# Order of the vector work around a seven-product down projection: two layers of a Trainium2 block stack

## The reference, cut to what matters

```python
def conv_ffn(h, w_up, conv_w, conv_b, w_down):
    up = h @ w_up
    a, bval = up[..., :D_FF], up[..., D_FF:]
    a = causal_conv3(a, conv_w) + conv_b
    return (jax.nn.silu(a) * bval) @ w_down      # 512 x 2816 by 2816 x 1024

for l in range(2):
    h = rms_norm(x, norm_mix[l]); proj = h @ w_in[l]
    ...                                          # attention, x = x + mixed @ w_out[l]
    h = rms_norm(x, norm_ffn[l])
    x = x + conv_ffn(h, w_up[l], conv_w[l], conv_b[l], w_down[l])
return rms_norm(x, norm_final)
```

## Time and profile before

| | us |
|---|---|
| median of three runs | 2137.65 |
| the profiled execution | 2137.98 |
| its span, first to last instruction | 2136.1 |
| TensorE busy in it | 2104.3 |
| VectorE busy in it | 1434.2 |
| ScalarE busy in it | 833.5 |

### The profile page before, as it was taken

How to read it: one execution, slowest core, us unless ns; L and a number is a source line. 1 busy time by engine, 2 the same in 40 slices (tenths; PEclk the granted TensorE clock), 3 DMA queues, 4 the chain that set the end, 5 groups by cost and what they waited for, 6 DMA issues and landing times.

```text
span 2136.1 us, 25152 instructions
## 1 busy us (share of the span) xinstructions
PE 2104.3 (99%) x10183; PEld 1733.5 (81%) x10183; DVE 1434.2 (67%) x1880; ACT 833.5 (39%) x1092; POOL 40.4 (2%) x67
## 2 busy tenths in 40 slices
PE   7999999999999999999999999999999999999998
PEld 4888888888888887888888888788788888888876
DVE  6899897953665748634856666964853476666696
ACT  3323232322352345344353333444544435333344
POOL 1000000000000100000000000000000000000000
PEclk9999999999999999999999999999999999999999
DMA  9432322332332232322234433853232223443385
GB/s 312 153 119 84 99 91 97 99 102 96 99 104 97 101 99 79 119 79 77 93 109 148 135 130 140 318 192 99 79 119 79 80 99 120 142 141 125 141 308 196
DMA packets 188855, 272.28 MB, mean 127 GB/s; under 512 B 5052, under 2 KB 154436, under 8 KB 187972
## 3 DMA queue, kind: packets, MB, share of 16 engines
q1 hardware_dynamic: 178432, 221.01, 30.8%
q0 software_dynamic: 4192, 27.84, 3.7%
q10 hardware_dynamic: 6116, 21.82, 2.7%
HBM read 244.96 MB, written 25.69 MB: 127 GB/s over the span
## 4 chain that ended last, share of the span: by engine, by line
PE 92%; DVE 5%; ACT 1%; issue 1%; DMA 0%; POOL 0%; SPq 0%; POOLq 0%; ACTq 0%; DVEq 0%
PE psum L2126 29%; PE psum L2128 29%; PE psum L2127 29%; DVE whl L577 1%; PE psum L2625 1%; PE psum L2657 1%; PE psum L2637 1%; PE psum L2355 1%; DMA ada<-in_w_ada 0%; PE psum L2580 0%; PE psum L2610 0%; PE psum L2596 0%; DVE mrow L1974 0%; PE psum L2150 0%; ACT hT L988 0%
## 5 line engine op out<-in xcount | busy, mean ns | idle before, releaser
L2126 PE MATMUL psum<-hT,whl 128*128 128x512 f32 (+1 forms) x2064 | 789.1, 382 | 2.7 <-DVE whl L577 1.4
L2128 PE MATMUL psum<-hT,whl 128*128 128x512 f32 (+1 forms) x2064 | 783.1, 379 | 0.0
L2127 PE MATMUL psum<-hT,whl 128*128 128x512 f32 (+1 forms) x2064 | 783.0, 379 | 0.0
L577 DVE TENSOR_TENSOR whl<-raw,whl 128x1024 fp32r<-128x1024 f32 x361 | 437.3, 1214 | 264.7 <-ACT whl L570 264.5
L570 ACT ACTIVATE whl<-raw 128x1024 fp32r<-128x1024 f32 x361 | 376.8, 1048 | 334.1 <-PE psum L2128 287.8
L2126 PEld LDWEIGHTS psum<-hT,whl 128*128 128x128 f32 x2064 | 388.1, 188 | 83.1 <-issue 6.7
L2128 PEld LDWEIGHTS psum<-hT,whl 128*128 128x128 f32 x2064 | 388.2, 188 | 73.5
L2127 PEld LDWEIGHTS psum<-hT,whl 128*128 128x128 f32 x2064 | 388.3, 188 | 71.7 <-issue 0.2
L2126 PE MATMUL psum<-whl,hT 128*128 128x512 f32 (+1 forms) x320 | 112.2, 351 | 1.9 <-DVE whl L577 1.9
L2127 PE MATMUL psum<-whl,hT 128*128 128x512 f32 (+1 forms) x320 | 111.0, 347 | 0.0
L2128 PE MATMUL psum<-whl,hT 128*128 128x512 f32 (+1 forms) x320 | 111.0, 347 | 0.0
(11 more groups left out here) (346 smaller groups left out, 2561.5 us busy)
## 6 DMA issues: line engine op xcount, KB each, us to landing
raw<-in_w_in SPq DMA_DIRECT2D x87, 1024.0 KB, 5.1
raw<-in_w_up SPq DMA_DIRECT2D x44, 1024.0 KB, 6.2
raw<-in_w_down SPq DMA_DIRECT2D x22, 1024.0 KB, 5.6
s_by_pair<-sstage POOLq DMA_DIRECT2D x22, 768.0 KB, 4.1
ff_r<-s_by_pair ACTq DMA_DIRECT2D x22, 768.0 KB, 6.5
raw<-in_w_branch SPq DMA_DIRECT2D x12, 1024.0 KB, 5.1
raw<-in_w_out SPq DMA_DIRECT2D x12, 1024.0 KB, 5.0
raw<-in_w_down SPq DMA_DIRECT2D x20, 512.0 KB, 5.5
```

The lines of the kernel that those rows point to most:

```text
L577: nc.vector.tensor_tensor(whl_view(w, 1), raw_view(w), whl_view(w, 0).bitcast(F), ALU.subtract).then_inc(w_lo, 1)
L2126: M(out_, stat_hi, mov_hi, start=start, stop=False, **kw)
L2127: M(out_, stat_hi, mov_lo, start=False, stop=False, **kw)
L2128: return M(out_, stat_lo, mov_hi, start=False, stop=stop, **kw)
```

## The change

It has five parts. The last pair's token sums leave the loop over `f2` and go between the stage's later pieces, on VectorE and on ScalarE. The two adds of banks 6 and 7 go ahead of `split_lo` of sD2. The order of splits and norm steps between the layers changes on both engines. TensorE's transposes of token block 3 go behind the first half tile of sq0 in layer 1, as they already did in layer 0. In the last row `statistics` moves ahead of the multiplication by the gain.

```diff
 # ScalarE, norm(s), s != 2
                     norm_hi(s, 0)
-                    if s != 4:
+                    if s == 4:
+                        split_hi(w0 + 4)
+                        scaled(s, 2)
+                        split_hi(w0 + 5)
+                        norm_hi(s, 1)
+                    else:
                         norm_sum(s, 2)
-                    scaled(s, 2)
-                    norm_hi(s, 1)
-                    split_hi(w0 + 4)
-                    split_hi(w0 + 5)
+                        ...
                     norm_sum(s, 3)
                     scaled(s, 3)
                     norm_hi(s, 2)
                     split_hi(w0 + 6)
                     split_hi(w0 + 7)
 # ScalarE, end of a turn of f2; tokens_hi and sums_hi hold the lines as they were
-                    act.wait_ge(s_sums, 2 * (PAIRS * l + f2) + 1)
-                    ...
+                    if f2 < PAIRS - 1:
+                        tokens_hi(f2)
+                        sums_hi(f2)
 # ScalarE, the stage
                 for w in range(W[("sB", l, 0)], W[("sD", l, 0)] + 1):
                     split_hi(w + 3)
+                    if key_of[w] == ("sB", l, 2):
+                        tokens_hi(PAIRS - 1)
+                        sums_hi(PAIRS - 1)
                     if key_of[w] in back_at:
                         sums_back(back_at[key_of[w]])
 # VectorE, gain0 and statistics (last layer only)
-                    step(V.tensor_scalar(ms0[:, tb:tb + 1], ...))
+                    ms0_at[tb] = step(V.tensor_scalar(ms0[:, tb:tb + 1], ...))
+                    if tb == 3:
+                        statistics(tb)
                     V.tensor_tensor(x[:, tb, 0:512], x[:, tb, 0:512], frow[:, 0:512], ALU.mult).then_inc(s_gain0, 1)
-                    dve.wait_ge(s_gain0, tb + 1)
+                    dve.wait_ge(dve_chain, ms0_at[tb])
 # VectorE, the stage; token_sums, tokens_lo and sums_lo hold the lines as they were
+                    if ahead == ("sD", l, 2):
+                        for i in range(2):
+                            dve.wait_ge(quad_full, 10 * l + 7 + i)
+                            add(i, 1, 6 + i).then_inc(quad_read, 1)
                     split_lo(w + 3)
                     if ahead[0] == "sA":
                         t3(l, ahead[2])
                     key = key_of[w]
+                    if key == ("sA", l, 2):
+                        token_sums(l, PAIRS - 1)
+                    elif key == ("sA", l, 3):
+                        sums_lo(l, PAIRS - 1)
+                    elif key == ("sA", l, 5):
+                        tokens_lo(l, PAIRS - 1)
                 ...
-                for i in range(2):
-                    dve.wait_ge(quad_full, 10 * l + 7 + i)
-                    add(i, 1, 6 + i).then_inc(quad_read, 1)
 # VectorE, between the layers
                 norm_lo(s, 0)
+                split_lo(w0 + 4)
+                split_lo(w0 + 5)
                 norm_lo(s, 1)
-                split_lo(w0 + 4)
                 whole_row(3)
-                split_lo(w0 + 5)
                 statistics(3)
                 gained(s, 2)
                 norm_lo(s, 2)
 # VectorE, end of a turn of f2
-                    V.tensor_tensor(fsil[:, 0, 256:], ...)
-                    ...
+                    if f2 < PAIRS - 1:
+                        token_sums(l, f2)
+                        tokens_lo(l, f2)
+                        sums_lo(l, f2)
 # TensorE, first_attention_tiles
                 value_rows(0)
                 value_rows(1)
-                transposed(s, 2 if s == 2 else 3)
+                if s == 2:
+                    transposed(s, 2)
                 half_tile(("sq", l, 0), 0)
-                if s == 2:
-                    transposed(s, 3)
+                transposed(s, 3)
                 half_tile(("sq", l, 1), 0)
```

More of the change, by code:

```diff
@@ L1175, in _, with tokens_hi, sums_hi @@
                 lead(lead_keys(("w_out_2", l, KT)))
+                def tokens_hi(f2):
+                    act.wait_ge(s_sums, 2 * (PAIRS * l + f2) + 1)
+                    for j in range(2):
+                        A(ff[:, 2 * f2 + j, 0, :], fsil[:, j, :], ACT.Copy).then_inc(ff_hi, 1)
+                def sums_hi(f2):
+                    act.wait_ge(s_sums, 2 * (PAIRS * l + f2) + 2)
+                    act.wait_ge(s_stored, 16 * (PAIRS * l + f2))
+                    A(sstage[:, 0, :], ssum[:], ACT.Copy).then_inc(s_hi, 1)
                 norm(s + 1)
@@ L1764, in t2, with token_sums, tokens_lo, sums_lo @@
                 V.tensor_tensor(b11, b11, t3_of(kk), ALU.add).then_inc(t2_done, 1)
+            def token_sums(l, f2):
+                await_read(dve, ("up_b", l, 2 * f2 + 1))
+                V.tensor_tensor(fsil[:, 0, 256:], fsil[:, 0, 256:], fsil[:, 1, 256:], ALU.add).then_inc(s_sums, 1)
+                if f2 == 0:
+                    dve.wait_ge(x_moved, 32 * l + 16)
+                    dve.wait_ge(s_xn, 4 * (2 + 2 * l) + 4)
+                dve.wait_ge(s_sums, 2 * (PAIRS * l + f2) + 1)
+                link(V.tensor_tensor(ssum[:, 0:256], fsil[:, 0, 256:], fsil[:, 0, 0:256], ALU.subtract))
+                V.tensor_tensor(ssum[:, 256:768].rearrange("p (a b) -> p a b", a=2), fsil[:, 1, :].rearrange("p (a b) -> p a b", a=2),
+                                ssum[:, 0:256].rearrange("p (a b) -> p a b", a=1).to_broadcast((P, 2, 256)), ALU.subtract).then_inc(s_sums, 1)
+            def tokens_lo(l, f2):
+                for j in range(2):
+                    f = 2 * f2 + j
+                    dve.wait_ge(ff_hi, FT * l + f + 1)
+                    V.tensor_tensor(ff[:, f, 1, :], fsil[:, j, :], ff[:, f, 0, :].bitcast(F), ALU.subtract).then_inc(ff_lo, 1)
+            def sums_lo(l, f2):
+                dve.wait_ge(s_hi, PAIRS * l + f2 + 1)
+                V.tensor_tensor(sstage[:, 1, :], ssum[:], sstage[:, 0, :].bitcast(F), ALU.subtract).then_inc(s_lo, 1)
             def t3(l, kk):
@@ L1788, in gain0 @@
                     dve.wait_ge(s_sq0, tb + 1)
-                    step(V.tensor_scalar(ms0[:, tb:tb + 1], ssq0[:, tb:tb + 1], 1.0 / D, LN_EPS, ALU.mult, ALU.add))
+                    ms0_at[tb] = step(V.tensor_scalar(ms0[:, tb:tb + 1], ssq0[:, tb:tb + 1], 1.0 / D, LN_EPS, ALU.mult, ALU.add))
+                    if tb == 3:
+                        statistics(tb)
                     V.tensor_tensor(x[:, tb, 0:512], x[:, tb, 0:512], frow[:, 0:512], ALU.mult).then_inc(s_gain0, 1)
+                ms0_at = {}
                 def statistics(tb):
@@ L1863, in quad_rows @@
                         gain0(tb)
-                        statistics(tb)
+                        if tb == 2:
+                            statistics(tb)
                         last_rows(tb)
```

## The result

Over 20 runs the changed kernel has a median of 2141.28 us, against 2137.68 us for the kernel before (20 runs): a ratio of 1.0017, with an interval of 1.0010 to 1.0024. It is slower by 3.6 us, just inside the 0.2% that was called no change, and it lies outside the stated range of 2133.2 to 2138.8. Its executions are also wide apart, from 2137.3 to 2143.9 us, where eighteen of the first kernel's twenty lie within 1.1 us of its median (the other two took 2339.55 and 3020.28 us). The profiled execution took 2142.86 us with a span of 2141.1.

What follows compares the result with a forecast made beforehand. TensorE, busy 2104.3 of 2136.1 us, was taken to bound the kernel. Terms -6.74 - 0.69 - 0.31 + 4.2 + 1.7 = -1.84 us gave 2136.14 from 2137.98, or 2135.8 on the median's side; range 2133.2 to 2138.8.

Steps and rivals of the forecast that it cites:

- Part 1, the last pair's sums: Start of the sA/sB/sC stage, both layers: moving the sums ends TensorE's waits and a slow-clock stretch, saving 6.74 us.
- No wait is left: sA to sC stages: after the sums move, TensorE waits for no low part of weights.
- VectorE's cover of 0.6 us: sB pieces: the thinnest lead of VectorE's low-part splits over TensorE's need, 0.6 us at sB5.
- the 6.74 us: Both layers' sA to sC stages: the saving claimed for moving the last pair's sums, 3.74 + 3.00 us.
- from about 13.7 us on it decides the sign: Load of pair 9: a landing about 13.7 us or more after issue would decide the forecast's sign.
- the -1.84: Whole kernel: the forecast change in us, all terms summed, against the profiled execution's 2137.98 us.
- Part 2, the adds: First sD product: the gap behind sC10 goes, 0.69 us a layer, counted as saved in layer 1 only.
- Part 3, the order between the layers: Value rows to sq1: TensorE waits 4.4 us before sq0 and 2.6 before sq1, 4.2 us lost.
- The clock: Behind the new waits between the layers: one fall of TensorE's clock, 1.7 us lost, bounds 0 to 3.4.
- Part 4, the last row: Last row: statistics starts earlier, ahead of the multiplication by the gain, 0.31 us saved.
- The rival with two falls of the clock: Between the layers: a clock fall behind each of the two waits, 2137.5 us; chance 0.15.
- the collision rival: sB stage: moved store and reload of x delay pair 9's load, TensorE waits 3.5 us a layer, 2146.2 us; chance 0.06.

Runs made afterwards that it cites:

- e10: Kernel before with only the last pair's sums moved, the reload of x in two parts and the last row's statistics wait shortened; 2131.14 us, ratio 0.9969.
- e1: Kernel before with only the last pair's sums moved, plus the last row's statistics wait shortened to the first sum; 2133.14 us, ratio 0.9981.
- e6: Changed kernel with the reload of x cut in two, 0.9 MB ahead of the last pair's store, 1.2 MB where it was; 2138.07 us, ratio 1.0001.
- e5: Changed kernel with unused half-width matmuls filling TensorE's waits before sq0's and sq1's half tiles (34 and 20); 2135.96 us, ratio 0.9994.
- e2: Kernel before with only the reordering between the layers, plus the shortened statistics wait; 2143.16 us, ratio 1.0030.
- e4: Changed kernel with GpSimd's reload of x issued once sB7 has been used, not sB3; 2140.87 us, ratio 1.0017.
- e8: Changed kernel with the last row's statistics behind the multiplication again, waiting on the first sum alone; one execution, 2140.34 us.
- e7: Changed kernel with the reload of x in two parts and the splits of sq0 and sq1 moved forward between the layers; 2127.31 us, ratio 0.9953.

## Why the prediction was wrong

**Part 1, the last pair's sums: right in mechanism, wrong in "No wait is left".** The waits at sA2 and sB2 went, VectorE's cover of 0.6 us held, and e10 gives the 6.74 us as 6.4 in the median (6.6 less the shortened wait) and 6.72 in its trace. The step that failed is the DMA side. I saw that the reload of x would start beside the loads of pairs 8 and 9, put a rival on it, and set its condition at 12 us from the issue of pair 9's load. It took 13.0 and 13.7 us:

```profile
raw<-in_w_down SPq DMA_DIRECT2D x1, 1024.0 KB, 13.0
...
raw<-in_w_down SPq DMA_DIRECT2D x1, 1024.0 KB, 13.7
```

The sum nevertheless had it at nothing. I argued that pair 8 is issued ahead of the reload, which is true of pair 8, and didn't carry the argument to pair 9, which is issued behind the reload in both layers, by 0.16 us in layer 0 (1360.22 and 1360.38). Moved by the 3 us that I gave it, the reload would have started ahead of pair 9's load too; it moved by 4.8 in layer 0. My mark "from about 13.7 us on it decides the sign" was wrong by my own terms as well: with a wait of the landing less 12 us in each layer, 0.92 us twice undo the -1.84, so the mark is 12.9. In the profiled execution the late load kept 1.5 us of layer 0's gain and 2.7 of layer 1's (there with a smaller wait at sC7, also behind a load). Over many runs it is 2.0 us for both layers (e1 against e10) or 3.2 (the changed kernel against e6), and it is a part of the spread.

**Part 2, the adds: right.** The gap before the first sD product is gone in both layers; two short waits for low parts, 0.19 and 0.33 us, stand among layer 0's sD products, where the first kernel had one of 0.32.

**Part 3, the order between the layers: right as to the order.** Forecast were waits of 4.4 and 2.6 us and a loss of 4.2; the trace has 4.29 and 2.54 idle, and e5 gives 4.1.

**The clock: the term that was mis-sized.** I took one fall at 1.7 us and allowed two, 3.4. The profiled execution has 10.2 us at the low level, and its stretch is 42.47 - 38.48 = 4.0 us longer than e5's. Over the runs, e5 against the changed kernel, it is 5.3 us in the median, which holds for the clock only if the loads' delays are equal in both; in the two profiles they are not (e5's stages take 1.7 us less), so 4 us is the safer figure. The executions themselves agree that the clock makes much of the spread: of the changed kernel's twenty, the six with a recorded mean clock of 0.998 take 2139.6 us on average, the eight with 0.997 take 2141.5, the five with 0.996 take 2143.0. Two errors stand behind the price. A fall need not last the 3.4 us of the one I had a row for: the first one here lasts 6.8. And the low clock came while sq0's tile and the transposes ran, on which `gained(3)` and sq1's split hang, so nothing hid it. The price of 1.7 us itself was also too plain, as e2 showed: the old fall hid a wait and cost 0.8. How often the clock falls isn't settled by the order of work: the same two waits have one fall of 3.4 us in the profiles of e2 and e4, and one of 6.8 with another of 3.4 in those of the changed kernel, e6 and e8. e4's stretch, with the one fall, takes 39.87 us, 1.4 more than e5's. Why the fall is longer in some executions stays open.

**Part 4, the last row: wrong, by a small term.** `statistics` starts 0.3 us earlier as forecast, but then the multiplication runs on VectorE beside GpSimd's power, which takes 0.38 us longer: 0.07 lost where 0.31 was to be gained. I had taken the power's 0.55 us as fixed. The shortened wait alone gains 0.18 (e8), and moving `statistics` gives 0.25 back.

**Together:** -1.84 forecast, +4.88 in the profiled execution. The loads account for 4.1 of the 6.7 us between the two, the clock for some 2.2, the last row for 0.4. The rival with two falls of the clock had the clock's side nearly right (3.4 us, against 4.0 in this profile), and the collision rival the other: landing less 12 us gives waits of 1.0 and 1.7 us, and TensorE waited 0.89 and 1.61; I had treated as exclusive two things that came together. The range held neither beside the other.

## What to carry to other kernels

Where work is moved off a stage's start, follow the DMAs that hang on it by the landing of every load in the crowded stretch, not of the first one. Before an instruction moves on one engine, list what the other engines have queued behind the one that waits for it: eight transposes moved by one tile held back a weight split with which they had nothing to do. A wait of TensorE costs its own length and, where it is long, can cost up to as much again in clock (here 4.1 us by order, and 1.4 to 4.0 of clock in the profiles). A wide spread of the runs is a sign of such a wait or of a load that lands about when it is needed: 6.6 us in the changed kernel, 0.14 in e7, which has neither.

## What the runs showed of the hardware

TensorE's clock: with gaps of 4.3 and 2.5 us idle, e2's profile has 3.4 us at 0.50, from 0.25 us before the end of the first gap on, and the changed kernel's has 6.8, from 1.4 us before its end on, and another 3.4, with the same order of work between the layers. With the gaps filled by matmuls that compute nothing it stayed at 1.00. The Trainium skill (TensorE: Matmul & The Clock Gate, Part 1) has the monitor run free of the program, with which these differences agree.

GpSimd's power on 128x1 words took 0.55 us alone (seven traces) and 0.93 (six) beside a 128x512 multiplication of VectorE. The Trainium skill (SBUF — State Buffer, SBUF: two separate sides) describes a port pair that the two share, held for a whole instruction, also against a VectorE instruction with two SBUF inputs; the trace agrees, as the power that started 0.16 us into the multiplication ended 0.4 us behind it.
